# Two layers of a hybrid encoder with a PEER layer: steps between the gathered rows moved, and some dots taken with normalised rows in PSUM

## The reference, cut to what matters

```python
h = rms_norm(x); p = h @ w_in                       # 1536 + 256 + 896 columns
x = x + concat(diff_attention(p), s5_mixer(p), rwkv7_mixer(p)) @ w_out
q = rms_norm(x) @ w_q                               # 8 heads x 2 x 128
s = einsum('thmd,hmkd->thmk', q, sub_keys)          # 128 keys per half
top_s, top_i = top_k(s, 16)                         # per half
best_s, best_pos = top_k(sums of 16 x 16 pairs, 16)
act = gelu(einsum('thkd,td->thk', u_tab[expert], hb))
x = x + einsum('thk,thkd->td', softmax(best_s) * act, v_tab[expert])
```

## Time and profile before

| | |
|---|---|
| median of 3 runs | 1837.36 us (1813.93 to 1841.94) |
| profiled execution | 1838.64 us, span 1836.8 us |
| PE, DVE, ACT, POOL busy | 74, 77, 21, 62% of the span |
| HBM read | 638.65 MB, 348 GB/s |
| mean granted TensorE clock | 0.885 |

### The profile page before, as it was taken

The page is one execution under the profiler, slowest core; times in us unless marked ns, Lnnn a source line. Parts: engine busy times, 40 slices in busy tenths (PEclk is TensorE's granted clock), DMA queues, the critical chain, the costliest instruction groups (busy, mean ns, idle before and its releaser), DMA issues. The chain is left out here.

```text
span 1836.8 us, 17575 instructions
## 1 busy us (share of the span) xinstructions
PE 1366.3 (74%) x5274; PEld 783.4 (43%) x5274; DVE 1418.5 (77%) x3427; ACT 383.6 (21%) x933; POOL 1133.0 (62%) x1046
## 2 busy tenths in 40 slices
PE   7889498687978388867888777967978837555557
PEld 6567354255456144334455363434546413222122
DVE  7867699997679669898668799887867875576653
ACT  2332221322111121322121221311221212001000
POOL 2002576777674756477657787576677766666664
PEclk9979699989899689989899989988999958978989
DMA  7348998999999998998999999999999999999998
GB/s 222 127 146 285 337 367 336 409 367 357 373 401 395 331 371 310 338 352 321 387 386 404 403 393 407 338 346 346 364 381 405 386 392 348 357 354 354 371 367 323
DMA packets 204723, 640.90 MB, mean 349 GB/s; under 512 B 18603, under 2 KB 35861, under 8 KB 204629
## 3 DMA queue, kind: packets, MB, share of 16 engines
q0 software_dynamic: 147920, 538.25, 77.0%
q1 hardware_dynamic: 56172, 100.96, 15.6%
q10 hardware_dynamic: 536, 0.57, 0.1%
HBM read 638.65 MB, written 1.05 MB: 348 GB/s over the span
## 5 line engine op out<-in xcount | busy, mean ns | idle before, releaser
L614 POOL DMA_INDIRECT arena<-in_peer_u_dram,expert x512 | 563.6, 1101 | 416.8 <-DVE expert L1768 150.3
L614 POOL DMA_INDIRECT arena<-in_peer_v_dram,expert x512 | 559.7, 1093 | 264.8 <-issue 152.4
L2393 PE MATMUL bank<-arena,diag 128*128 128x512 f32 x768 | 443.1, 660 | 269.2 <-DMA arena<-in_peer_v_dram,expert 122.2
L1806 DVE SCALAR_TENSOR_TENSOR arena<-arena,normed 128x1024 f32<-128x1024 f32 x364 | 434.1, 1224 | 70.5 <-DMA arena<-in_peer_u_dram,expert 53.7
L2394 PE MATMUL bank<-arena,diag 128*128 128x512 f32 x768 | 426.6, 637 | 7.3 <-issue 6.9
L2393 PEld LDWEIGHTS bank<-arena,diag 128*128 128x128 f32 x768 | 141.0, 205 | 474.4 <-issue 408.2
L2394 PEld LDWEIGHTS bank<-arena,diag 128*128 128x128 f32 x768 | 158.3, 206 | 213.9 <-issue 213.9
L1804 DVE SCALAR_TENSOR_TENSOR arena<-arena,bank 128x1024 f32<-128x1024 f32 x148 | 175.7, 1219 | 77.5 <-DMA arena<-in_peer_u_dram,expert 46.5
L1038 ACT ACTIVATE diag<-ident,weight 128x128 f32<-128x128 f32 x384 | 128.6, 391 | 235.6 <-DVE weight L1823 101.2
L1881 PE MATMUL bank<-h_cm,wring 128*128 128x128 f32 x1152 | 150.0, 291 | 32.0 <-issue 20.2
L1881 PEld LDWEIGHTS bank<-h_cm,wring 128*128 128x128 f32 x1152 | 146.1, 207 | 45.6 <-issue 37.5
(11 more groups left out here) (443 smaller groups left out, 1573.3 us busy)
## 6 DMA issues: line engine op xcount, KB each, us to landing
wring<-in_w_in_dram SPq DMA_DIRECT2D x40, 1024.0 KB
wring<-in_peer_w_q_dram SPq DMA_DIRECT2D x25, 1024.0 KB
wring<-in_w_out_dram SPq DMA_DIRECT2D x16, 1024.0 KB
arena<-in_peer_u_dram,expert POOLq DMA_INDIRECT x512
arena<-in_peer_v_dram,expert POOLq DMA_INDIRECT x512
arena<-in_peer_w_q_dram SPq DMA_DIRECT2D x7, 1024.0 KB, 10.7
wring<-in_w_in_dram SPq DMA_DIRECT2D x4, 512.0 KB
x<-in_x_dram SPq DMA_DIRECT2D x2, 512.0 KB, 5.6
```

Source lines behind the costliest of these rows:

```text
L614: nc.gpsimd.indirect_dma_start(out=rows[g % RING], out_offset=None, in_=tables[kind], in_offset=bass.IndirectOffsetOnAxis(ap=expert[:, n % ...
L1806: ins = stt(row, row, 1.0, hb, ALU.mult, ALU.mult, accum_out=dots[:, slot:slot + 1])
L2393: mm(bank[6][:, :], d, row[:, 0:512], start=first, stop=end)
```

## The change

The steps stand at other rows in all four tables of ROWS_BY. Those that the prediction speaks of:

| beside unit | step: row before, row after |
|---|---|
| 0 | p3 139, 147; d3 146, 158; p4 155, 162; d4 156, 163; p5 156, 163; d5 160, 168; p6 162, 168; d6 165, 169; sa 167, 173; q6 232, 232; q7 233, 241 |
| 1 | late_t3a 30, 24; late_t3b 35, 29; late_t3c 35, 31; late_id3 38, 40; bc1 38, 29; bc2 38, 38; bc3 45, 41; bc4 46, 45; y 165, 176; yd 169, 176; mean 169, 178; dev, var, vara, outd 170, 178; out3 173, 184; q0 188, 187; q1 189, 187 |
| 2 | y 157, 163; yd 157, 163; mean 160, 163; dev 160, 164; q0 187, 187; q1 189, 187; s0 189, 187; t0a 200, 190 |
| 3 | late_t3a 44, 27; late_t3b 44, 40; late_t3c 52, 41; late_id3 60, 41; late_t4a 92, 77; late_t4b 93, 95; late_t4c 113, 95; late_id4 133, 95 |

c2 and u6 are now at 137 and 169 beside unit 0, 127 and 151 beside unit 1, 122 and 145 beside unit 2, and c1 at 125, 123 and 105.

The dots of the rows from c2 to u6 now take the normalised rows from PSUM banks 4 and 5, in units 0 to 2. ACT copies them there after `tokens`. The scores move from banks 3 and 4 to 2 and 3, the update of the inverse's transpose from bank 2 to 0, the transposed probabilities from bank 5 to 2, and these come later:

```diff
-        hb_psum = {0: bank_all[:, 6:8, :], UNITS - 1: bank_all[:, 0:2, :]}
-        HB_COPIES = {0: 2, UNITS - 1: 4}
+        hb_early, hb_beside, hb_last = bank_all[:, 6:8, :], bank_all[:, 4:6, :], bank_all[:, 0:2, :]
+        BESIDE = [[q for q in range(rows_by["c2"], rows_by["u6"]) if ORDER[q][0] == 0] for rows_by in ROWS_BY[:UNITS - 1]] + [[]]
         def dot_in_psum(n, q):
-            return n == UNITS - 1 or n == 0 and q < LEAD
+            if n == UNITS - 1:
+                return hb_last, 2 * UNITS + 2
+            if n == 0 and q < LEAD:
+                return hb_early, 2
+            if q in BESIDE[n]:
+                return hb_beside, 2 * n + 4
+            return None, 0
...
 # ACT, beside the levels
                     if k == 1:
                         tokens()
+                        act.wait_ge(all_masked, n + 1)
+                        normed_copied(n - 1, hb_beside)
                     if k == 2:
                         softmax(0)
                     if k == 4:
-                        turned_probs(0)
                         softmax(1)
                     if k == 6:
+                        turned_probs(0)
                         turned_probs(1)
...
 # DVE, gather
-                        if kind == 0 and dot_in_psum(n, q):
-                            if q == 0:
-                                dve.wait_ge(hb_ok, HB_COPIES[n])
-                            ins = stt(row2, row2, 1.0, hb_psum[n], ALU.mult, ALU.mult, accum_out=dots[:, slot:slot + 1])
+                        view, copies = dot_in_psum(n, q)
+                        if kind == 0 and view is not None:
+                            if q == 0 or q in BESIDE[n][:1]:
+                                dve.wait_ge(hb_ok, copies)
+                            ins = stt(row2, row2, 1.0, view, ALU.mult, ALU.mult, accum_out=dots[:, slot:slot + 1])
...
 # PE
-                    pe.wait_ge(comb_ok, 2 * n + hp + 1)
+                    pe.wait_ge(comb_ok, 2 * n + (2 if n else hp + 1))
...
                     pe.wait_ge(rhs_ok, n + 1)
+                    if n and BESIDE[n - 1]:
+                        row_used(pe, ROWS * (n - 1) + BESIDE[n - 1][-1])
...
                     if k == 3:
                         score_pair(1)
+                    if k == 5:
                         turn_probs(0)
-                    if k == 5:
+                    if k == 6:
                         turn_probs(1)
```

More of the change, by code:

```diff
@@ L106 @@
     {
[6 rows of a table removed]
-        "tanh": 100, "glud": 103, "gss": 104, "abkr": 108, "mats": 108, "masked": 119, "p1": 123, "c1": 125,
[3 rows of a table removed]
-        "yd": 172, "mean": 175, "dev": 180, "var": 181, "vara": 185, "outd": 196, "out3": 196, "xm": 196, "fsq":
[4 rows of a table removed]
-    {
[4 rows of a table removed]
-        86, "glu": 89, "tanh": 92, "glud": 92, "gss": 102, "abkr": 102, "mats": 102, "masked": 111, "p1": 116,
[3 rows of a table removed]
-        "y": 165, "yd": 169, "mean": 169, "dev": 170, "var": 170, "vara": 170, "outd": 170, "out3": 173, "xm":
[4 rows of a table removed]
-    {
[4 rows of a table removed]
-        77, "glu": 78, "tanh": 78, "glud": 91, "gss": 91, "abkr": 91, "mats": 91, "masked": 97, "p1": 101, "c1":
[3 rows of a table removed]
-        157, "yd": 157, "mean": 160, "dev": 160, "var": 160, "vara": 160, "outd": 165, "out3": 165, "xm": 169,
[4 rows of a table removed]
-    {
-        "exp0": 6, "gate0": 15, "late_t3a": 44, "late_t3b": 44, "late_t3c": 52, "late_id3": 60, "exp3": 69,
-        "gate3": 80, "late_t4a": 92, "late_t4b": 93, "late_t4c": 113, "late_id4": 133, "exp4": 145, "gate4": 156},
[6 rows of a table added]
+        97, "tanh": 100, "glud": 103, "gss": 104, "abkr": 108, "mats": 109, "masked": 119, "p1": 123, "c1": 125,
[3 rows of a table added]
+        "yd": 180, "mean": 181, "dev": 181, "var": 191, "vara": 196, "outd": 196, "out3": 198, "xm": 198, "fsq":
[4 rows of a table added]
+    {
[4 rows of a table added]
+        83, "glu": 91, "tanh": 91, "glud": 97, "gss": 106, "abkr": 109, "mats": 109, "masked": 114, "p1": 118,
[3 rows of a table added]
+        "y": 176, "yd": 176, "mean": 178, "dev": 178, "var": 178, "vara": 178, "outd": 178, "out3": 184, "xm":
[4 rows of a table added]
+    {
[4 rows of a table added]
+        80, "glu": 81, "tanh": 83, "glud": 91, "gss": 91, "abkr": 91, "mats": 91, "masked": 99, "p1": 105, "c1":
[3 rows of a table added]
+        163, "yd": 163, "mean": 163, "dev": 164, "var": 167, "vara": 169, "outd": 178, "out3": 178, "xm": 178,
[4 rows of a table added]
+    {
+        "exp0": 0, "gate0": 0, "late_t3a": 27, "late_t3b": 40, "late_t3c": 41, "late_id3": 41, "exp3": 44,
+        "gate3": 71, "late_t4a": 77, "late_t4b": 95, "late_t4c": 95, "late_id4": 95, "exp4": 95, "gate4": 108},
 )
@@ L335, in score_banks @@
             kv, at = P * (n % TILES + 1), 256 * pairs[0] if n == 0 else 0
-            return bank[3 + m if n else (4, 3)[m]][:, at:at + 2 * kv * len(pairs)].rearrange("p (a k) -> p a k", k=kv)
+            return bank[2 + m if n else (4, 3)[m]][:, at:at + 2 * kv * len(pairs)].rearrange("p (a k) -> p a k", k=kv)
         def score_bank(n, g):
@@ L775, in turned_probs @@
                     aT = probs[:, 1, 2 * hp:2 * hp + 2, 0:kv].rearrange("p a (c t) -> p c a t", t=P)
[L776 removed]
+                    A_(aT, bank[2 if n else 5][:, 0 if n else 256 * hp:2 * kv if n else 256 * hp + 256].rearrange("p (c a t) -> p c a t", a=2, t=P),
                        ACT.Copy).then_inc(aT_ok, 1)
@@ L966, in mixing, with normed_copied @@
                 deviation()
-            def normed_copied(n):
+            def normed_copied(n, view):
                 act.wait_ge(f_h, n + 1)
                 for i in range(2):
-                    A_(hb_psum[n][:, i, :], normed[:, n % 2, 512 * i:512 * i + 512], ACT.Copy).then_inc(hb_ok, 1)
+                    A_(view[:, i, :], normed[:, n % 2, 512 * i:512 * i + 512], ACT.Copy).then_inc(hb_ok, 1)
             def peer(n, layer, t):
@@ L1012, in peer @@
                     if n == 0 and g == 0:
-                        normed_copied(0)
+                        normed_copied(0, hb_early)
             def choosing(n):
@@ L1054, in _ @@
                 if n == UNITS - 1:
-                    normed_copied(n)
+                    normed_copied(n, hb_last)
                 for step in by_rows(n, choosing(n), unit_steps(n + 1)):
@@ L1493, in level_done @@
                         own(tt(inv[:, :, :], inv[:, :, :], quad(1), ALU.add))
-                    tt(invT[:, :, :], invT[:, :, :], quad(2), ALU.add).then_inc(up_ok, 1)
+                    tt(invT[:, :, :], invT[:, :, :], quad(0 if n else 2), ALU.add).then_inc(up_ok, 1)
                     dve.wait_ge(up_ok, NL * n + k)
@@ L1973, in turn_probs @@
                         for j in range(2):
-                            last = tr(quad(5)[:, 2 * (c if n else hp) + j, :], probs[:, 0, 2 * hp + j, P * c:P * c + P], ident[:, :])
+                            last = tr(quad(2 if n else 5)[:, 2 * (c if n else hp) + j, :], probs[:, 0, 2 * hp + j, P * c:P * c + P], ident[:, :])
                     last.then_inc(aT_ps, 1)
@@ L2100, in level_update @@
                             mm(quad(1)[:, i, :], invT[:, i, :], prod[:, i, :], start=True, stop=True)
-                        last = mm(quad(2)[:, i, :], prod[:, i, :], invT[:, i, :], start=True, stop=True)
+                        last = mm(quad(0 if n else 2)[:, i, :], prod[:, i, :], invT[:, i, :], start=True, stop=True)
                     last.then_inc(up_ps, 1)
```

1 line of the change is left out of this document (removed), and 70 rows, old and new, of the table ROWS_BY.

## The result

The changed kernel took 1874.58 us (1874.36 to 1899.22, 3 runs) against 1837.36 us (1813.93 to 1841.94, 3 runs), 37 us more by the medians. The ratio of the fast runs alone is 1.0291, with a 95% interval of 1.0218 to 1.0364, which would be 53 us on 1837 (40 to 67). It is slower beyond doubt of the measurement, and the two profiled executions lie 36 us apart. The forecast was 1823, the range 1794 to 1852.

What follows compares the result with a forecast made beforehand. End set by 168 us start, 1271 gather issuing, 159 lengthened gathers, 226 waits, about 13 tail; the change acts on lengthened gathers and waits. Terms sum to -15.5 from 1838.64: 1823 us, range 1794 to 1852 (own 1808 to 1834).

Steps and rivals of the forecast that it cites:

- Dots from PSUM: Rows c2 to u6, units 0 to 2: 40 dots reading PSUM shorten POOL's gathers, -5 us, between 0 and -14.5.
- Copies: Six ACT copies to PSUM behind `tokens`: 0 us, up to 3.5 if ACT doesn't wait for PE there.
- probabilities: Later transposes of the probabilities put one more PE-ACT round trip ahead of `attend`: +3 us for three units, 0 to +6.
- q7, -9.5: Unit 0's last query chunk, row 233 to 241: weight load and product no longer stack, -9.5 us, between 0 and -19.
- Unit 1's rows 24 to 66: Late t3 steps and phase doublings spread over more rows, cutting 14.8 us of POOL waits: -8 us, 0 to -15.
- Unit 3, -5: Late t3 and t4 steps lumped on rows 40, 41 and 95: -5 us net, between -20 and +12.
- Bunched chains: Chains p4 to d6 (unit 0) and y to outd (unit 1) let DVE idle: +5 and +3 us, 0 to 8.55 each.
- the slower rival: Three bunches stall DVE beyond 12.3 us, 33 us, plus 12 for unit 3's lumps: 1861 us, chance 0.15.
- a ring that covers 12.3: POOL's gathers wait for the row 15 places before; 15 x 1.24 us less a 6.39 us landing covers 12.3 us.
- t0a of unit 2: Step moved from row 200 to 190, DVE waits some 9 us for scores, mostly covered: +1 us, 0 to +9.
- signs of being wrong: POOL less busy but waiting as much longer; waits over 8 us at units 0's or 1's bunches; unit 3 over 370 us.
- unit 3's idle time: Some 12 and 7.5 us of DVE idle at unit 3's t3 steps, unexplained by the profile; 7.5 assumed per new lump.

Runs made afterwards that it cites:

- set 3: Runs on one faster chip, kernel before 1742.38 us: among them the changed kernel, 1757.5 us, and its code with the old tables, 1737.19 us.
- set 1: Four runs on one slower chip, kernel before 1844.78 us: changed kernel 1.0327, tables alone 1.0197, code alone 1.0085, changed kernel with SBUF dots and no copy waits 1.0237.
- code-only kernel: The changed kernel with the four old tables of rows, so only the new code, on a slower chip: 1858.24 us, 1.0085 against the kernel before.

## Why the prediction was wrong

On chips like the case's the ratio of 1.0291 is the tables' 2.0% and the 0.8 to 0.9% of the PSUM dots with their two waits; nothing else shows. (The 37 us between the medians would be 2.0% alone; the shares belong to the ratio.) By the steps of the prediction:

- **Dots from PSUM, -5 us (0 to -14.5).** POOL's share came out as forecast in the case, 7.0 us less busy, but that is less than two profiles of one kernel can differ by. The sign of the bound was wrong. Where no signal is late they win 5 to 11 us; on the chips of the case they cost 14 to 15 with their two waits. I allowed no loss, because the dots take DVE the same time; the other user of what they set free, the gathers' own traffic, was not asked about. Part of the term's reasoning failed on the better chip too: I counted nothing where DVE is full, but slowed gathers cost their whole 26 us there, all three units together. The Trainium skill (SBUF — State Buffer, Who interferes with whom) infers that `tensor_tensor` takes only the read interface and descriptor generation needs the write interface. Carried over to these dots, which are another instruction, that would leave the gathers alone, and the traces do not agree: POOL was busy for 14.6 us less with the dots from PSUM. They fit the same section's rule that two SBUF inputs contend with a GpSimd instruction that reads SBUF, if a gather's reading of its indices from `expert` counts as one; no run here tells that reading from the descriptors.
- **Copies 0, probabilities +3.** Not contradicted: 1.0003, which is 0.6 us with 6 either way.
- **q7, -9.5.** About right: 6.64 + 13.51 became 7.50 + 2.39 in the case, 10 us less; on the other kind the 9.47 us wait became one of 5.03. No run put q7 back alone.
- **Unit 1's rows 24 to 66, -8.** The 10.70 us wait went. On the other kind of chip there was nothing to win: the old table has no wait over 3.5 us at these rows in set 3, the new one has one of 4.30. The unit as a whole lost on both.
- **Unit 3, -5.** The unit lasts 370.3 us for 369.7, in the case's two profiles. Behind the lump on row 95 stands a wait of 12.99 us, not 7.5, and it took all that the earlier rows won. On the other kind of chip the unit does win, 2 us.
- **Bunched chains, +5 and +3.** In unit 0 the wrong chain. p4 to d6 on rows 162 to 169, on which the slower rival rested as well, cause no wait over 2 us on the chips without late signals; the 7.13 us of the case's chip stand at row 173, 15 behind u3 and d3, with the late signal shown above. In unit 1 the chain y to outd on rows 176 to 178 shows on the case's kind only: DVE's dots hold POOL up at rows 191 and 193 for 8.19 us in the case and for 5.99 and 9.86 in set 1, where the kernel before had 8.55 at row 185; on the other kind row 193 waits 2.75 to 5.22.
- **What had no term.** da1 to da4 on row 74 beside unit 0: 8.8 us, on the other kind of chip. It is the kind of place I had priced in unit 3, 14.8 us of DVE work in one lump against a ring that covers 12.3; I had listed the steps that came near a wait known from the trace before, and not asked of the whole new table which rows hold more than 12.3 us. And in unit 1 the key chunks, of which I wrote that I hold them "inside the bunched chains' term": the wait there is 10 to 14 us (7.16 in the kernel before, in the case), of which at most a few are lost in the end. Other places without a term were never put back by themselves. da steps stand behind rows 87 and 88 of unit 1 (8.02 and 11.20 us in set 3, against 3.69 and 9.95 at rows 86 and 90 with the old table) and behind row 76 of unit 2 (13.29, against 8.98 at row 69). In unit 0, q0 and q1, now both on row 200, keep PE at their products for 9.98 us, and row 216 waits 7.88 us, where the old table has no wait over 3.5 in the same set.
- **t0a of unit 2, +1.** The unit's table costs 5 us on the second kind, with no wait at t0a; the largest is at row 76, behind the da steps (12.12 us above, in the case).

The step that failed is thus the sum over the tables: -9.5 - 8 - 5 + 8 + 1 = -13.5 us, measured +36 (1.0197 and 1.0198) on chips like the case's and +23 (1.0099 / 0.9969) on the others; and next to it the bound of the PSUM dots. What the runs show in its place is lumps of DVE and PE work, the da steps above all, on rows whose work I had not added up; only 8.8 us of them are shown by a run that undoes one. The rival that ended on the slower side, 1861, had the sign and 22 of the 36 us between the profiles, but mainly for places that did not decide. Of the signs of being wrong, POOL less busy with longer waits came true, and unit 3 at 370.3 us.

**What stays open.** Why the tables cost 13 us more on the one kind of chip; no single table was run there, so the places above are shown for the other kind and only seen in the traces of the case's. Of the 23 us there, too, 10 to 14 are put down to no single place by a run. And whether it is the gathers' pace that makes PE's signals late. For it: the 407 against 336 GB/s, the share of late increments, which rises with the traffic, and that the code with the PSUM dots hurts on the one kind of chip alone. Against its being enough: none is late on the other kind at the same traffic. And the kernel that slows the gathers with the PSUM dots in place never ran on a chip with late signals, nor did SBUF dots with both waits kept; that the waits cost 15 us there is made unlikely by the second kind, where the code with both waits is no slower than the kernel before (0.9969), and is not excluded.

## What to carry to other kernels

When steps are moved over a schedule whose slack is a ring, add up the work of every row of the new table and compare each lump with what the ring covers; the waits of the old trace only tell where the old table was tight. A change that removes a brake from a transfer should get a loss as a bound too, when the transfers already take 97% of the DMA time: here it lost on one kind of chip, by a mechanism that is not shown. And a wait that the profile can't name ("remote" in a program on one core) belongs neither to the old table nor to the new one: find out whether it is there on another chip before building a term on it, as I built unit 3's idle time.

## What the hardware showed that I had not expected

- The same kernel took 1836 to 1845 us on some chips and 1741 to 1742 on others, 5.4 to 6.0% apart, with a granted TensorE clock of 0.87 to 0.89 in the profiles of the first kind and 0.89 to 0.91 in those of the second.
- On the slower chips PE's release reaches DVE up to 17 us after the matmul's record ends: 16.82 us above, 46.8 us in four waits in the code-only kernel. PE works on meanwhile, and there the four increments held up came within 0.3 us. In none of the twelve profiles of the faster chips is there one such wait. In the one followed closely it came as the gathers' traffic ebbed from 401 GB/s, in the case's own with 387 still moving.
- One change had opposite signs on the two: the new code with the old tables cost 0.8% on the one (1.0085, 1.0049 to 1.0121) and won 0.3% on the other (0.9969, 0.9956 to 0.9981).
